# Loads of the state-space block, and the splitting of the first down weights, moved into the tail of the block in front

## The reference

```python
def hybrid_layer(x, w_in, conv_w, ..., w_out, ln_g, ln_b):
    proj = jnp.einsum("bld,de->ble", x, w_in)
    q, k, v, z_attn, z_ssm, xbc, dt_raw = jnp.split(proj, IN_SPLITS, axis=-1)
    attn = sliding_window_attention(q, k, v, sinks) * jax.nn.silu(z_attn)
    xbc = jax.nn.silu(causal_depthwise_conv(xbc, conv_w, conv_b))
    xs, bm, cm = jnp.split(xbc, [D_INNER, D_INNER + N_SSM_GROUPS * D_STATE], axis=-1)
    ...
    y = ssd_chunked(xs, dt, a, bm, cm)
    ...
    ssm = gated_rmsnorm(y, z_ssm, ssm_norm_w)
    out = jnp.einsum("ble,ed->bld", jnp.concatenate([attn, ssm], axis=-1), w_out)
    return layer_norm_2(DEEPNORM_ALPHA * x + out, ln_g, ln_b)

def channel_mix(h, w_up, ffn_dw_w, ffn_dw_b, w_down):      # in the first layer
    z = causal_dwconv(h @ w_up, ffn_dw_w, ffn_dw_b)
    z_gate, z_val = jnp.split(z, 2, axis=-1)
    return (jax.nn.silu(z_gate) * z_val) @ w_down
```

## Time and profile before

| | kernel before |
|---|---|
| median of 3 runs | 3341.51 us |
| the profiled execution, its own time | 3339.61 us |
| its span in the profile | 3337.8 us |
| TensorE busy | 3075.4 us, 92% |
| VectorE, ScalarE, GpSimd busy | 1552.5, 1104.6, 984.9 us |
| granted TensorE clock, mean of the span | 0.96 |
| DMA | 308.57 MB, mean 92 GB/s |

### The profile page before, as it was taken

How to read it: one execution, slowest core, us unless ns; L and a number is a source line. 1 busy time by engine, 2 the same in 40 slices (tenths; PEclk the granted TensorE clock), 3 DMA queues, 4 the chain that set the end, 5 groups by cost and what they waited for, 6 DMA issues and landing times. The chain is left out here.

```text
span 3337.8 us, 50028 instructions
## 1 busy us (share of the span) xinstructions
PE 3075.4 (92%) x21074; PEld 2436.7 (73%) x21074; DVE 1552.5 (47%) x2316; ACT 1104.6 (33%) x1885; POOL 984.9 (30%) x638
## 2 busy tenths in 40 slices
PE   5999799795999998998999999789989999996898
PEld 3886489674888887887877777567778777775676
DVE  3999745434332333244034433378431434424875
ACT  3012333233222222123134434455222444445532
POOL 2442022202333333332233333142223333331421
PEclk8999899897999999999999999899999999998999
DMA  5112400032111111122212112576431122127754
GB/s 205 45 51 85 150 4 4 27 114 95 50 45 49 50 45 40 51 98 89 70 46 82 64 62 84 186 221 186 148 105 52 50 71 82 51 76 261 203 160 140
DMA packets 341929, 308.57 MB, mean 92 GB/s; under 512 B 11328, under 2 KB 300480, under 8 KB 337248
## 3 DMA queue, kind: packets, MB, share of 16 engines
q1 hardware_dynamic: 266944, 242.63, 23.0%
q10 hardware_dynamic: 74784, 63.05, 5.7%
HBM read 248.89 MB, written 54.66 MB: 91 GB/s over the span
## 5 line engine op out<-in xcount | busy, mean ns | idle before, releaser
L1871 PE MATMUL PS<-x_high_sb,w_high_sb 128*128 128x512 f32 x1312 | 530.0, 404 | 0.0
L1871 PE MATMUL PS<-x_high_sb,w_low_sb 128*128 128x512 f32 x1312 | 518.2, 395 | 0.0
L1871 PE MATMUL PS<-x_low_sb,w_high_sb 128*128 128x512 f32 x1312 | 517.4, 394 | 0.0
L1871 PEld LDWEIGHTS PS<-x_high_sb,w_high_sb 128*128 128x128 f32 x1312 | 247.0, 188 | 76.0 <-issue 23.9
L1871 PEld LDWEIGHTS PS<-x_high_sb,w_low_sb 128*128 128x128 f32 x1312 | 246.9, 188 | 57.7
L360 PE MATMUL PS<-h_high_sb,up_high_sb 128*128 128x512 f32 x704 | 274.8, 390 | 13.5 <-POOL up_low_sb L1436 13.5
L1871 PEld LDWEIGHTS PS<-x_low_sb,w_high_sb 128*128 128x128 f32 x1312 | 247.3, 189 | 52.3
L1486 DVE SCALAR_TENSOR_TENSOR z_sb<-PS,cols_sb,z_sb 128x1023 f32<-128x1023 f32 x88 | 112.8, 1282 | 348.5 <-ACT z_sb L1467 342.1
L360 PE MATMUL PS<-h_low_sb,up_high_sb 128*128 128x512 f32 x704 | 274.6, 390 | 0.0
L360 PE MATMUL PS<-h_high_sb,up_low_sb 128*128 128x512 f32 x704 | 274.4, 390 | 0.0
L2109 DVE CUSTOM_DVE_ANT_0 scores_sb<-PS,alibi_sb,sinks_sb 128x256 f32<-128x256 f32 (+1 forms) x256 | 104.4, 464 | 342.2 <-PE PS L1889 342.2
(11 more groups left out here) (405 smaller groups left out, 6090.0 us busy)
## 6 DMA issues: line engine op xcount, KB each, us to landing
w_raw_sb<-w_in SPq DMA_DIRECT2D x102, 512.0 KB, 3.7
up_raw_sb<-w_up SPq DMA_DIRECT2D x44, 512.0 KB, 3.7
ada_slots_sb<-ada_w SPq DMA_DIRECT2D x16, 1024.0 KB, 6.7
attn_raw_sb<-attn ACTq DMA_DIRECT2D x32, 512.0 KB, 5.9
decays_sb<-running_sums SPq DMA_DIRECT2D x16, 1024.0 KB, 7.4
attn_raw_sb<-state_out ACTq DMA_DIRECT2D x32, 512.0 KB, 4.0
xbc<-staged_sb ACTq DMA_DIRECT2D x24, 512.0 KB, 2.6
xbc_sb<-xbc SPq DMA_DIRECT2D x16, 768.0 KB, 9.0
```

The costliest lines, as they stand in the source:

```text
L1871: last = pe.matmul(PS[:, bank, :], a[:, n % 2, k], b[:, k, cols], start=k == 0 and a is WH and b is HH, stop=k == KT - 1 and a is WL)
```

## The change

1. The up projection's tail loads the first two down weight pieces into the buffer `gate_or_weights` and GpSimd splits them into slot 0 of the up weight parts, which become part of the down projection's slots. The down projection starts at step 2 with its loads and splits. Its raw buffer is that same `gate_or_weights`, and so the load of the next layer's first weight tile waits for the last split.
2. The row stores of the down projection and of the first hybrid layer are no longer awaited at their block's end. Semaphores `rows_stored` are awaited by SP in the state-space block ahead of its loads of residual rows, and by ScalarE ahead of its first write of a q tile (that buffer holds the stored rows).
3. The buffers XB (xbc chunks), AA (attention chunks) and YS are allocated for the whole layer and shared with RAW, BIAS and KH of the attention block. In its tail SP loads the eight first weight pieces (four loads of 512 KB, as the keys come free), xbc chunks 0 and 1, and attention chunk 0. The store of the last attention group is cut in two halves. At the block's end neither attention nor gate stores are awaited; SP and ScalarE wait for them in the next block ahead of the loads that read them.
4. In the state-space block SP's order starts with rows 0; ScalarE casts attention chunk 0 first, and `move(0)` and `masked(0)` come after four of the eight first pieces.

```diff
 def up_projection(...)
+            for q in range(2):
+                sp.dma_start(first_raw[:, q], t.w_down[q * P:(q + 1) * P, 0:NH]).then_inc(first_loaded[q], 16)
...
+            pool.wait_ge(s.tile_done, 2 * FT + 1)
+            for q, parts in enumerate((WH, WL)):
+                high, low = (parts[:, 0].rearrange("p (a b) n -> p a (b n)", a=2)[:, a] for a in range(2))
+                pool.wait_ge(first_loaded[q], 16)
+                nc.gpsimd.tensor_copy(high, first_raw[:, q]).then_inc(s.high, 1)
+                pool.wait_ge(s.high, 2 * FT + q + 1)
+                nc.gpsimd.tensor_tensor(low, first_raw[:, q], high, ALU.subtract).then_inc(first_split, 1)
 def down_projection(...)
+            sp.wait_ge(split, 2 * FT)
             ahead.load(sp)
             for k in range(TT):
                 sp.wait_ge(s.out, k + 1)
-                sp.dma_start(dst[k * P:(k + 1) * P], X[:, k]).then_inc(s.stored, 16)
-            sp.wait_ge(s.stored, 16 * TT)
+                sp.dma_start(dst[k * P:(k + 1) * P], X[:, k]).then_inc(dst_stored, 16)
...
-            for i in range(len(steps)):
+            for i in range(2, len(steps)):
 def projections_and_attention(...)
-        KH = alloc(m, ctx, "k", [P, 4, T])
+        KH = land.YS
-        RAW = alloc(m, ctx, "w_raw", [P, 3, KT, P])
+        RAW = land.XB[:].rearrange("p a k n -> p (a k n)").rearrange("p (s k n) -> p s k n", s=3, k=KT)
-        BIAS = alloc(m, ctx, "alibi", [P, 2, G4, 2 * P])
+        BIAS = land.AA[:].rearrange("p a (g b) n -> p a g (b n)", g=G4)
...
+            sp.wait_ge(s.scored, 2 * TT)
+            first_weights(0)
+            first_weights(2)
+            for i in range(2):
+                sp.wait_ge(stage[i], 16 * sum(slot[j] == i for j in staged if j[0] == "xbc"))
+            sp.wait_ge(s.split, len(jobs))
+            for c in range(2):
+                sp.dma_start(land.XB[:, c], xbc_d[:, :, c * P:(c + 1) * P].rearrange("k p t -> p k t")
+                             ).then_inc(land.xb_in[c], 16)
+            sp.wait_ge(s.stored, 16 * (KVH - 1))
+            sp.wait_ge(land.half_stored, 16)
+            sp.wait_ge(s.biased, TT * (KVH - 1))
+            sp.dma_start(land.AA[:, 0], attn_d[:, :, 0:P].rearrange("k p t -> p k t")).then_inc(land.aa_in[0], 16)
+            sp.wait_ge(s.scored, N)
+            first_weights(1)
+            first_weights(3)
...
+                elif kind == "q" and i == 0:
+                    act.wait_ge(src_stored, 16 * TT)
...
+                if u == N - TT // 2 + 2:
+                    store_last_attention(0)
+            store_last_attention(1)
-            act.wait_ge(s.stored, 16 * KVH)
             act.wait_ge(step.s.row_out, 16)
-            act.wait_ge(stage[0], 16 * sum(slot[j] == 0 for j in staged if j[0] in ("xbc", "zs")))
-            act.wait_ge(stage[1], 16 * sum(slot[j] == 1 for j in staged if j[0] in ("xbc", "zs")))
 def state_space_and_mix(...)
-            inputs(0)
-            sp.dma_start(skip[:], d_skip.to_broadcast([P, SH])).then_inc(s.skip_in, 16)
-            first_weights(0)
-            first_weights(1)
+            sp.wait_ge(src_stored, 16 * TT)
+            rows(0)
+            sp.dma_start(skip, d_skip.to_broadcast([P, SH])).then_inc(s.skip_in, 16)
             residual(0)
-            rows(0)
+            rows(1)
             residual(1)
-            rows(1)
-            inputs(1)
             rate_rows(1)
+            for signal, count in gates_stored:
+                sp.wait_ge(signal, count)
             for i in range(KT, KT + 4):
                 weights(i)
             rows(2)
             gates(0)
+            sp.wait_ge(land.rest_stored, 16)
             residual(2)
...
-            load(0)
+            high(0)
             load(1)
-            move(0)
-            high(0)
             for i in range(KT):
+                if i == KT // 2:
+                    move(0)
                 first(i)
```

More of the change, by code:

```diff
@@ L1496, in _, with down_projection @@
                                     Z[:, 1], ALU.mult).then_inc(s.mid, 1)
-def down_projection(m, MID, GM, src, dst, ahead):
+def down_projection(m, MID, GM, src, dst, ahead, dst_stored, W0, RAW, raw_in, split):
     nc, t, PS = m.nc, m.t, m.PS
@@ L1507, in down_projection, with weights @@
         ML = alloc(m, ctx, "mid_low", [P, SLOTS, T], F32R)
-        RAW = alloc(m, ctx, "down_raw", [P, 2, NH])
-        WH = alloc(m, ctx, "down_high", [P, SLOTS, NH], F32R)
-        WL = alloc(m, ctx, "down_low", [P, SLOTS, NH], F32R)
+        W2 = alloc(m, ctx, "down_parts", [P, 2, NH], F32R)
+        W0 = [parts[:].rearrange("p q (a b) n -> p q a (b n)", a=2) for parts in W0]
+        def weights(i, part):
+            slot = i % SLOTS
+            return W0[slot % 2][:, slot // 2, part] if slot < SLOTS - 1 else W2[:, part]
+        WH, WL = (lambda i: weights(i, 0)), (lambda i: weights(i, 1))
         X = MID[:, 0:TT]
-        s = phase(m, "raw0 raw1 x_in high low whigh split used prod moved eps sq based rooted inverse scaled chain out "
-                     "stored")
-        raw_in = [s.raw0, s.raw1]
+        s = phase(m, "x_in high low whigh used prod moved eps sq based rooted inverse scaled chain out")
         block = ctx.enter_context(nc.Block())
@@ L1772, in tensor_ends, with projections_and_attention @@
         pe.transpose(self.m.PS[:, 3, 0:TT * SH], self.NA[:], self.m.const("ident")).then_inc(self.s.turned, 1)
-def projections_and_attention(m, layer, w, sinks, HH, HL, x, step, attn_d, xbc_d, gate_d, primed):
+def projections_and_attention(m, layer, w, sinks, HH, HL, x, step, attn_d, xbc_d, gate_d, primed, land, w_out, src_stored):
     nc, t, PS = m.nc, m.t, m.PS
@@ L2166, in _ @@
                     gate(u - 1)
+    gates_stored = [(stage[i], 16 * sum(slot[j] == i for j in staged if j[0] in ("xbc", "zs"))) for i in range(2)]
+    return gates_stored
 def state_space_and_mix(m, layer, d_skip, xbc_d, gate_d, rows_d, attn_d, y_d, src, w, ln_g, ln_b, dst, ahead,
-                        DT, A, NA, EI, DE, CD):
+                        DT, A, NA, EI, DE, CD, land, gates_stored, src_stored, dst_stored):
     nc, t, PS, X = m.nc, m.t, m.PS, m.HT
@@ L2181, in state_space_and_mix @@
     with ExitStack() as ctx:
+        XB, AA, YS, raw = land.XB, land.AA, land.YS, land.pieces
         RS = alloc(m, ctx, "inverse_rms", [P, 2, HD])
-        XB = alloc(m, ctx, "xbc", [P, 2, XT, P])
         ZS = alloc(m, ctx, "z_gate", [P, KT, P])
@@ L2849, in hybrid_kernel @@
     weights = [Ahead(m, shared.rearrange("p (k n) -> p k n", k=KT), i, t.w_in_2[i], O_K) for i in range(LAYERS)]
-    first_block(m, shared, x_mid, x1, weights[0])
+    rows_stored = [nc.alloc_semaphore(f"rows_stored_{i}") for i in range(LAYERS)]
+    first_block(m, shared, x_mid, x1, weights[0], rows_stored[0])
     m.HT = alloc(m, m.ctx, "HT_2", [P, KT, T])
     recycle(m)
-    second_layer(m, 0, x1, x2, weights[0], weights[1])
+    second_layer(m, 0, x1, x2, weights[0], weights[1], rows_stored[0], rows_stored[1])
     recycle(m)
-    second_layer(m, 1, x2, t.out, weights[1], None)
+    second_layer(m, 1, x2, t.out, weights[1], None, rows_stored[1], None)
     m.ctx.close()
```

103 lines of the change are left out of this document (63 added, 40 removed).

## The result

| | before | after |
|---|---|---|
| median | 3341.26 us (4 runs, 3340.16 to 3341.56) | 3309.29 us (4 runs, 3307.14 to 3310.31) |
| ratio, 95% interval | | 0.9906 [0.9893, 0.9918] |
| profiled execution, its own time (span) | 3339.61 (3337.8) us | 3310.31 (3308.5) us |
| TensorE busy | 3075.4 us, 92% | 3067.4 us, 93% |
| granted clock, mean of the span | 0.96 | 0.963 |

The change takes 32.0 us off by the medians, 29.3 by the two profiled spans. Forecast were 45.9 us and 3295.6 us, in a range of 3283 to 3309. The time lies 0.3 us above the range's upper edge, and 2.7 above rival 1's 3306.6, the nearest of the cases.

The account below looks back on a forecast made before the run. TensorE was taken to bound the kernel, except at its seams, where transfers do. Terms 3.7 + 5.2 + 37.0 = 45.9 us off 3339.6 gave 3293.7, plus 1.9 for the median: 3295.6 us, range 3283 to 3309.

Parts of the forecast that it names:

- rival 1: State-space start: attention chunks on ScalarE's queue land in 18 us beside SP's backlog; gain 13 per layer, 3306.6 us; chance 0.23.
- Up to down: Seam from up to down projection: first weight parts made in the tail, VectorE's subtraction comes last; gain 3.7 us, bounds 3.0 to 5.0.
- Stores: Seams block to layer and layer to layer: wait for the last row store moves to its readers; 2.6 us each, 5.2 in all.
- What stays is 1.6: At those two seams, issue, drain and barrier remain: 4.25 less a store's 2.6 us landing, 1.6 us.
- Rival 3: Block ends drain transfers in flight, so stores are not handed over; 5.2 and twice 3 us lost, 3306.8 us; chance 0.07.
- The cover in the tail: Attention's tail: 4.19 MB of loads take 12.3 us within 16 to 28 us left, landing by about 2118 at no cost.
- The start at 2129.4: Attention to state space: without the wait for the last store, the next block starts at 2129.4, 3.7 us earlier.
- From the first fill to the intra-chunk product: State-space start: units 0 and 1, then chunk 2 after 12.7 us; product at 2155 to 2157 against 2175.08, 18 to 20 us.
- 18.5 a layer: Seam attention to state space, up to the third xbc chunk: gain 18.5 us per layer, 37.0 for both, outer bounds 13 and 24.4.
- Transfers as the second limit: State-space start: third xbc chunk queues behind all loads, 13.4 MB in 40.9 us, to 2170.3; gain 16.5 us.
- rival 2: State-space start is free because the chunks land early; 24.4 us per layer, 3283.8 us; chance 0.07.

Follow-up runs that it names:

- the experiment: The changed kernel with the row stores awaited again at the end of their own blocks (down projection, first hybrid layer); 3309.05 us, ratio 0.9909.
- chunk2_on_sp: Changed kernel plus attention chunk 1 loaded in the tail, third residual load issued later, attention chunk 2 loaded by SP instead of ScalarE; 3292.18 us, ratio 0.9862.

## Why the prediction was right or wrong

- **Up to down, 3.7 us: right.** Idle 8.34 us (forecast 8.4), released by mid_low. The seam shows 3.71, not the 3.0 worked out beside the page "SBUF — State Buffer", section "SBUF: two separate sides", of the Trainium skill. The trace doesn't test that rule: GpSimd's first operation of the block started at 1295.85, behind the first mid_low, which released TensorE at 1295.31.
- **Stores, 2.6 us a seam: right, a little high.** 2.1 and 2.3 between the two profiles, 2.3 and 2.3 in the experiment. "What stays is 1.6" came out as 1.95 us behind VectorE's last operation (2429.31 less 2427.36, and the same in the first layer) of 4.25 before; so 2.3 us went, and not the landing's whole 2.6. Rival 3 falls.
- **The cover in the tail: right.** No wait for xbc or first weights is left; the two xbc chunks land after 6.1 us and the first two weight loads after 6.0 (medians), under matmuls (busy 29.12 of 30 us).
- **The start at 2129.4: right.** The first transposes come 1.36 us behind the last attention product, the first fill 4.46 us behind it (2123.19 less 2118.73), as forecast.
- **From the first fill to the intra-chunk product: wrong, and this is the step that failed.** The forecast went "unit 0 until 2138 and unit 1 until 2144" with no landing for chunk 1 at all, a term put at nothing without a reason, and took over 12.7 us for chunk 2 from a stretch where SP's queue carried other loads. Unit 1 at 2138 needed chunk 1 at 2135.7 (a cast and a subtraction ahead of it, 2.3 us); on the clock of before, which is 9.41 us on here (2128.14 less 2118.73), it came at 2147.0. The wait of 11.04 us put the intra-chunk product 36.4 us behind the end of attention (2155.16 less 2118.73), against 27 to 29 forecast and 46.9 before: 10.5 us of gain for 18 to 20. The third xbc chunk, at 9.3 and 12.3 us of gain, is 9.2 and 6.2 under the 18.5 a layer. That is the size of the miss: 15.4 us on this term, of 16.6 between the forecast's 45.9 and the profiled pair's 29.3 (13.9 by the medians).
- **Rival 1 named it.** "Attention chunks go on ScalarE's queue in 512-byte rows beside SP's backlog", landing 18 us (measured 17.5 and 16.7), 13 us a layer (9.3 and 12.3), 3306.6 us (3309.3). It had it starve chunk 2, where it was chunk 1, and was given 0.23; that its time came nearest is in part luck, as it had the wrong chunk. What the experiments add is the law of it, and that the forecast could have had it: the 308 packets to 309 lie in the profile of before. Chunk 1's 1024 packets of 512 bytes beside 1024 of 4 KB are 4.7 MB, 13.8 us at 341 GB/s, and with some 3 us around it 17 us, an estimate (measured: 4.37 MB in 12.4 us, and 5.1 around it). In the forecast's own chain, 2129.4 and 17 and 2.3 for cast and subtraction, unit 1 would have begun at 2148.7 and not at 2138, 10.7 us later; 11.04 us of wait were measured. The Trainium skill says it too, page "DMA: Bandwidth & Descriptors", section "Queues, rings and completion order": an engine takes the queues in turn, a whole packet from each. The trace of the changed kernel agrees, with 1370 packets to 1375, where what the profile counts as a packet is one row. The 1040 to 381 beside eight small loads agree only if SP's queue was at times empty, which no run here shows.
- **Transfers as the second limit: right in kind.** The forecast had the third xbc chunk bound by the transfers; it is, with 3.70 us in the changed kernel and 6.3 once the attention chunks come in time, so none of these orders reaches the free start of rival 2 (24.4 a layer) at the third xbc chunk. Up to the intra-chunk product chunk2_on_sp has nearly all of it, 23.9 us (46.9 to 23.05). It has 38.85 and 38.81 us from attention's end to the third xbc transposes, gains of 19.8 and 20.5: the forecast's 18.5 and a little, and with it a time of 3292.

Left open: whether requesting the third xbc chunk earlier would win its 6 us (its buffer comes free only with the products on chunk 0), and why the packets of two queues go in bursts where SP's loads are small. Neither was tried.

## What to carry to other kernels

When work is moved ahead of a transfer, list which load each step then waits for, with a landing for each; a step without one is the one that fails. A landing doesn't carry over from one stretch to another: where two queues are busy, count packets, not bytes, and a load of short rows on a second queue goes at the pace of the long rows beside it. Here it paid to put what was needed first on the queue that held the backlog, ahead of it, rather than on a queue of its own.

## What the runs showed of the hardware

- Two busy queues shared by packets, one for one, whatever their bytes (1370 to 1375, 937 to 941, 1038 to 1028, 308 to 309, and 1068 to 1039 with short packets on both). The exception is a queue with eight loads of 192 KB one behind the other, 381 to 1040.
- One load of 512 KB in 512-byte rows landed after 4.6 or 4.7 us alone or first on its queue, 5.4 and 5.7 beside small loads in rows of its own size, 8.1 beside loads in short rows, 8.3 beside one load of 1024 KB, and 16.7 to 19.0 beside a backlog in long rows.
- A block's end (barrier and cleared semaphores) doesn't wait for transfers in flight: 2.3 us each at two seams.
- Whole times of kernels that differ only in these transfers scatter by 1.3 to 18.2 us between runs of one kernel, and the kernel before by 1.4 us in four runs and 9.0 in seven others; seams were told apart by idle time in the profile.
